# A decoder trunk on one core: slot counting, the router by token halves, and half of the gather ahead

## The reference

```python
def hierarchical_moe(h, w_rg, w_re, w_gate, w_up, w_down):
    t = h.reshape(-1, D)
    g_logits = (t @ w_rg).astype(F32)
    g_sel = jnp.argmax(g_logits, axis=-1)
    ...
    top_v, top_i = lax.top_k(e_in, TOP_K_IN_GROUP)
    e_w = jax.nn.softmax(top_v, axis=-1) * g_w
    ids = g_sel[:, None] * EXPERTS_PER_GROUP + top_i
    gates = jnp.einsum('nk,nke->ne', e_w, jax.nn.one_hot(ids, N_EXPERTS, dtype=F32))
    hg = jnp.einsum('nd,edf->nef', t, w_gate)
    hu = jnp.einsum('nd,edf->nef', t, w_up)
    act = (jax.nn.silu(hg.astype(F32)) * hu.astype(F32) * gates[..., None]).astype(t.dtype)
    y = jnp.einsum('nef,efd->nd', act, w_down)
    return y.reshape(B, S, D).astype(h.dtype)
```

## Time and profile before

| what | value |
|---|---|
| median of 3 runs | 1021.76 us (1020.68 to 1021.91) |
| the profiled execution | 1021.73 us |
| its span in the trace | 1019.8 us |
| mean granted TensorE clock | 0.996 of full speed |
| TensorE busy | 999.2 us, 98% of the span |
| VectorE busy | 477.2 us, 47% |
| DMA, mean over the span | 288 GB/s |

### The profile page before, as it was taken

One profiled execution on the slowest core, in us unless ns is written; L12 is line 12 of the kernel. 1 busy time (PEld: TensorE's weight loads), 2 busy tenths in 40 slices (PEclk: granted clock), 3 DMA queues, 4 the chain that ended last, 5 costly groups with the idle time before them and its releaser, 6 DMA issues.

```text
span 1019.8 us, 11159 instructions
## 1 busy us (share of the span) xinstructions
PE 999.2 (98%) x4494; PEld 547.1 (54%) x4494; DVE 477.2 (47%) x814; ACT 136.4 (13%) x323; POOL 98.8 (10%) x123
## 2 busy tenths in 40 slices
PE   8999999999999999999999999999999999999996
PEld 7657555669575454333334855565975433333332
DVE  2533375766554224432444636566655544444424
ACT  2211000411010010101112000032120010111111
POOL 3051032000010000000000512210000100000000
PEclk9999999999999999999999999999999999999999
DMA  9973000963379999999999420067385799999995
GB/s 359 425 299 131 35 0 6 409 249 123 125 277 391 406 423 421 419 423 420 421 420 420 163 82 1 1 254 285 148 327 193 297 421 420 421 420 421 421 415 220
DMA packets 44826, 293.58 MB, mean 288 GB/s; under 512 B 5472, under 2 KB 5728, under 8 KB 13024
## 3 DMA queue, kind: packets, MB, share of 16 engines
q1 hardware_dynamic: 38000, 266.36, 64.3%
q10 hardware_dynamic: 5616, 22.24, 5.6%
q0 software_dynamic: 1152, 4.19, 1.1%
HBM read 283.33 MB, written 9.44 MB: 287 GB/s over the span
## 4 chain that ended last, share of the span: by engine, by line
PE 89%; SPq 5%; DMA 3%; DVE 2%; issue 1%; POOL 0%; ACT 0%; DVEq 0%; POOLq 0%
PE bank L1001 18%; PE bank L1075 10%; PE bank L590 8%; PE bank L620 6%; PE bank L789 5%; PE bank L622 5%; PE bank L600 5%; PE bank L843 5%; PE bank L907 5%; SPq L512 5%; PE bank L693 5%; PE bank L1036 5%; PE bank L715 3%; DMA ring<-in_w_experts 3%; PE bank L580 2%; PE bank L877 1%
## 5 line engine op out<-in xcount | busy, mean ns | idle before, releaser
L1001 PE MATMUL bank<-ring,hT 128*64 128x512 f32 x704 | 195.0, 593 | 0.0
L1001 PEld LDWEIGHTS bank<-ring,hT 128*64 128x64 f32 x704 | 62.5, 137 | 87.2 <-issue 86.9
L590 PE MATMUL bank<-ring,hT 128*128 128x512 f32 x192 | 84.4, 592 | 0.0
L1937 DVE TENSOR_TENSOR x<-bank,x 128x512 f32<-128x512 f32 x64 | 44.3, 692 | 54.5 <-PE bank L1036 54.5
L1955 DVE TENSOR_SCALAR xs<-xs 128x512 f32<-128x512 f32 x8 | 3.4, 426 | 124.0 <-ACT xs L1315 124.0
L1036 PE MATMUL bank<-PT 128*128 128x512 f32 x128 | 59.2, 605 | 0.0
L1075 PE MATMUL bank<-ring,Vx 128*64 128x512 f32 x160 | 57.1, 596 | 1.4 <-DMA ring<-in_w_experts 1.3
L590 PEld LDWEIGHTS bank<-ring,hT 128*128 128x128 f32 x192 | 35.6, 190 | 40.2 <-issue 40.2
L1075 PE MATMUL bank<-ring,xs 128*64 128x512 f32 x224 | 56.7, 595 | 0.0
L600 PE MATMUL bank<-hT,ring 128*128 128x256 f32 x256 | 55.7, 379 | 0.8 <-DVE hT L1586 0.8
L789 PE MATMUL bank<-ring,hT 128*128 128x512 f32 x128 | 56.3, 595 | 0.1
(11 more groups left out here) (296 smaller groups left out, 1559.2 us busy)
## 6 DMA issues: line engine op xcount, KB each, us to landing
ring<-in_w_experts SPq DMA_DIRECT2D x146, 1024.0 KB, 15.0
ring<-in_w_mix SPq DMA_DIRECT2D x60, 1024.0 KB, 14.5
work<-in_w_experts SPq DMA_DIRECT2D x20, 1024.0 KB, 12.7
late<-in_w_experts SPq DMA_DIRECT2D x10, 1024.0 KB, 18.1
late<-in_w_mix ACTq DMA_DIRECT2D x4, 2048.0 KB, 10.0
keys<-in_w_experts SPq DMA_DIRECT2D x8, 1024.0 KB, 21.9
rot<-by_slot ACTq DMA_DIRECT2D x14, 512.0 KB, 8.0
by_slot<-late ACTq DMA_DIRECT2D x1, 4096.0 KB, 38.3
```

Of the source, the lines that this page charges most:

```text
L590: last = nc.tensor.matmul(b[:, :], lhs[:, c, m * P:(m + 1) * P], w[:, c, :], start=(c == 0), stop=(c == C - 1))
L1001: last = nc.tensor.matmul(banks[2 + g][b2 * CAP:(b2 + 1) * CAP, :], rows_T_of(p)[:, c, b2 * CAP:(b2 + 1) * CAP], w, start=(c == 0), stop=( ...
```

## The change

It has four parts.

1. The places of the first half are found as soon as its choice is there: one small matmul in a bank of its own (`rank0`, a new job) stands before p_3's last chunk and waits for `chosen` of half 0. VectorE scales the first half of `xs` at once, adds the base, and makes `slotf` and `hot` of half 0 ahead of the second choice (`slots`, `first_hot`, semaphore `r_first`).
2. The second half counts its places from the top end of each expert's 64 downwards (`top16` minus the count), so it doesn't need the first half's count; three matmuls are left in `rank`.
3. The gather is split by halves: the matmuls of half 0 run before and behind the `rank` matmuls, those of half 1 stay where the gather was. `keep_busy` gives one matmul in two places instead of two matmuls.
4. ScalarE's `first_loads` goes. The wait for the scatters stands behind the count of the first half slots and of gate, before pair 0's exponential, and the row loads of pairs 1 and 2 behind that exponential.

```diff
@@ job_list @@
-    jobs += [..., ("p_2", "D"), ("rt0", "D"), ("p_3", "D"), ("t5_10", "D"), ("t5_11", "D"), ("rt1", "D")]
+    jobs += [..., ("p_2", "D"), ("rt0", "D"), ("rank0", "D"), ("p_3", "D"), ("t5_10", "D"), ("t5_11", "D"), ("rt1", "D")]
@@ tensor @@
                 logits(0)
-                p_seventh("p_3")
+                NE = N_EXPERTS
+                p_seventh("p_3", range(3))
+                pe.wait_ge(chosen_done, 2 * L + 1)
+                b = open_bank(L, "rank0")
+                close(nc.tensor.matmul(b[:, 0:NE], before[:, :], chosen[:, 0, :], start=True, stop=True))
+                p_seventh("p_3", range(3, 4))
+
+                def gather(m, c2):
+
+                    b = banks[FIRST_ROWS[c2]]
+                    for k in range(4):
+                        last = nc.tensor.matmul(b[:, k * P:(k + 1) * P], xs[:, m, (4 * c2 + k) * P:(4 * c2 + k + 1) * P], hot[:, m, :],
+                                                start=(m == 0 and k == 0), stop=(m == 1 and k == 3), skip_group_check=True)
+                    return last
...
-                if L + 1 == DEPTH:
-                    wait_emptied(pe, L, BANK_BEFORE["router_kv0"])
-                keep_busy(2)
                 router_kv(0, range(2, 6))
+                pe.wait_ge(normed, 6 * L + 5)
+                pe.wait_ge(r_first[L], 1)
+                gather(0, 0)
+                keep_busy()
                 pe.wait_ge(chosen_done, 2 * L + 2)
                 b = open_bank(L, "rank")
-                NE = N_EXPERTS
-                nc.tensor.matmul(b[:, 0:NE], before[:, :], chosen[:, 0, :], start=True, stop=True)
-                nc.tensor.matmul(b[:, NE:2 * NE], before[:, :], chosen[:, 1, :], start=True, stop=False)
-                nc.tensor.matmul(b[:, NE:2 * NE], ones[:, :], chosen[:, 0, :], start=False, stop=True)
-                nc.tensor.matmul(b[:, 2 * NE:3 * NE], ones[:, :], chosen[:, 0, :], start=True, stop=False)
-                close(nc.tensor.matmul(b[:, 2 * NE:3 * NE], ones[:, :], chosen[:, 1, :], start=False, stop=True))
-
+                nc.tensor.matmul(b[:, 0:NE], before[:, :], chosen[:, 1, :], start=True, stop=True)
+                nc.tensor.matmul(b[:, NE:2 * NE], ones[:, :], chosen[:, 0, :], start=True, stop=False)
+                close(nc.tensor.matmul(b[:, NE:2 * NE], ones[:, :], chosen[:, 1, :], start=False, stop=True))
+
+                gather(0, 1)
+                keep_busy()
                 router_kv(0, range(6, C))
                 router_kv(1)
-                keep_busy(2)
...
                 for c2 in range(2):
-                    for k in range(4):
-                        for m in range(M):
-                            cols = xs[:, m, (4 * c2 + k) * P:(4 * c2 + k + 1) * P]
-                            last = nc.tensor.matmul(banks[FIRST_ROWS[c2]][:, k * P:(k + 1) * P], cols, hot[:, m, :], start=(m == 0), stop=(m == M - 1))
-                    routed_job(last)
+                    routed_job(gather(1, c2))
@@ scalar @@
-                def first_loads():
-                    act.wait_ge(r_sent[L], 16 * 2 * M)
-                    for p in (1, 2):
-                        load_rows(p)
-
...
                     units_read(p, "gate")
+                    if p == 0:
+                        act.wait_ge(r_sent[L], 16 * 2 * M)
                     nc.scalar.activation(rexp_of[L], banks[2][:, :], ACT.Exp, scale=-1.0).then_inc(r_gexp[L], 1)
+                    if p == 0:
+                        for q in (1, 2):
+                            load_rows(q)
                     units_read(p, "up")
...
-                either_way(act, L, routed, dense, first_loads, None, None, dense_last)
+                either_way(act, L, routed, dense, None, None, None, dense_last)
@@ vector @@
                 choose(0)
+                scale_tile(L, 2, 0)
+                wait_job(dve, L, "rank0")
+                emptied(V.tensor_tensor(rank[:, 0, :], base16, bank("rank0")[:, 0:N_EXPERTS], ALU.add))
                 p_sum("p_3", (1, 1))
...
+                wait_emptied(dve, L, "rank0")
+                slots(0)
                 wait_emptied(dve, L, "p_3")
                 rows_T("t5", 1, 24)
-                for m in range(M):
-                    scale_tile(L, 2, m)
+                scale_tile(L, 2, 1)
+                first_hot(0, r_first[L])
                 choose(1)
...
-                emptied(V.tensor_tensor(rank[:, :, :], bk[:, 0:2 * N_EXPERTS].rearrange("p (m n) -> p m n", m=M),
-                                        base16.unsqueeze(1).to_broadcast([P, M, N_EXPERTS]), ALU.add))
+                emptied(V.tensor_tensor(rank[:, 1, :], top16, bk[:, 0:N_EXPERTS], ALU.subtract))
                 wait_emptied(dve, L, "rank")
                 V.tensor_copy(most, mostf)
...
+                slots(1)
                 dve.sem_inc(flag_done, 1)
...
+                first_hot(1, r_hot[L])
```

More of the change, by code:

```diff
@@ L75, in job_list @@
     jobs += [(f"p_{i}", "D") for i in (7, 6, 5, 4)]
-    jobs += [("t5_00", "D"), ("t5_01", "D"), ("p_2", "D"), ("rt0", "D"), ("p_3", "D"), ("t5_10", "D"), ("t5_11", "D"), ("rt1", "D")]
+    jobs += [("t5_00", "D"), ("t5_01", "D"), ("p_2", "D"), ("rt0", "D"), ("rank0", "D"), ("p_3", "D"), ("t5_10", "D"), ("t5_11", "D"), ("rt1", "D")]
     return jobs + [("rank", "D")]
@@ L250, in trunk @@
         sm = sb("sm", [P, 112])
-        wsm = sb("wsm", [P, 242])
+        wsm = sb("wsm", [P, 258])
         early = PT[:, 2, 6:8, :].rearrange("p a t -> p (a t)")
@@ L346, in trunk @@
         r_hot = per_layer("r_hot")
+        r_first = per_layer("r_first")
         r_rowsT = per_layer("r_rowsT")
@@ L459, in trunk @@
         most = wsm[:, 241:242].bitcast(I32)
+        top16 = wsm[:, 242:258]
         one2 = PT[:, 1, 0, 0:64].rearrange("p (m k n) -> p m k n", m=M, k=2)
@@ L1883, in _, with slots, first_hot @@
                 choose(0)
+                scale_tile(L, 2, 0)
+                wait_job(dve, L, "rank0")
+                emptied(V.tensor_tensor(rank[:, 0, :], base16, bank("rank0")[:, 0:N_EXPERTS], ALU.add))
                 p_sum("p_3", (1, 1))
+                def slots(m):
+                    link(V.tensor_tensor(pick[:, m, :, :], one2[:, m, :, :], rank[:, m, :].unsqueeze(1).to_broadcast([P, 2, N_EXPERTS]), ALU.mult))
+                    link(V.tensor_reduce(slotf[:, m, :], pick[:, m, :, :], AX, ALU.add))
+                def first_hot(m, done):
+                    link(V.tensor_scalar(hot1[:, m, :], columns[:, :], slotf[:, m, 0:1], None, ALU.is_equal))
+                    V.scalar_tensor_tensor(hot[:, m, :], columns[:, :], slotf[:, m, 1:2], hot1[:, m, :], ALU.is_equal, ALU.add).then_inc(done, 1)
+                wait_emptied(dve, L, "rank0")
+                slots(0)
                 wait_emptied(dve, L, "p_3")
                 rows_T("t5", 1, 24)
-                for m in range(M):
-                    scale_tile(L, 2, m)
+                scale_tile(L, 2, 1)
+                first_hot(0, r_first[L])
                 choose(1)
@@ L1895, in _ @@
                 bk = bank("rank")
-                V.tensor_reduce(mostf, bk[:, 2 * N_EXPERTS:3 * N_EXPERTS], AX, ALU.max)
-                emptied(V.tensor_tensor(rank[:, :, :], bk[:, 0:2 * N_EXPERTS].rearrange("p (m n) -> p m n", m=M),
-                                        base16.unsqueeze(1).to_broadcast([P, M, N_EXPERTS]), ALU.add))
+                V.tensor_reduce(mostf, bk[:, N_EXPERTS:2 * N_EXPERTS], AX, ALU.max)
+                emptied(V.tensor_tensor(rank[:, 1, :], top16, bk[:, 0:N_EXPERTS], ALU.subtract))
                 wait_emptied(dve, L, "rank")
                 V.tensor_copy(most, mostf)
-                link(V.tensor_tensor(pick[:, :, :, :], one2[:, :, :, :], rank[:, :, :].unsqueeze(2).to_broadcast([P, M, 2, N_EXPERTS]), ALU.mult))
-                link(V.tensor_reduce(slotf[:, :, :], pick[:, :, :, :], AX, ALU.add))
+                slots(1)
                 dve.sem_inc(flag_done, 1)
                 V.tensor_copy(sloti, slotf[:, :, :].rearrange("p m k -> p (m k)")).then_inc(r_slots[L], 1)
-                inner = Chain(dve, r_chain[L])
-                for m in range(M):
-                    last = V.tensor_scalar(hot1[:, m, :], columns[:, :], slotf[:, m, 0:1], None, ALU.is_equal)
-                inner.link(last)
-                for m in range(M):
-                    last = V.scalar_tensor_tensor(hot[:, m, :], columns[:, :], slotf[:, m, 1:2], hot1[:, m, :], ALU.is_equal, ALU.add)
-                last.then_inc(r_hot[L], 1)
+                first_hot(1, r_hot[L])
                 dve.wait_ge(lexp_done, 2 * L + 2)
```

9 lines of the change are left out of this document (5 added, 4 removed).

## The result

The changed kernel took **1026.27 us** (median of five, 1025.4 to 1028.3) against 1021.91 for the kernel before it on the same chip: a ratio of 1.0042, 95% interval 1.0031 to 1.0054. That is 4.4 us slower, outside the predicted range. The profiled execution took 1027.07 us for a span of 1025.2.

A forecast was written before the change was run, and what follows sets the result against it. TensorE was taken to bound all before layer 1's end, the weight stream that end. 0.4 + 0.1 + 1.4 - 2.4 + 0.8 = +0.3 on 1021.73 gave 1022.0 us, range 1019.6 to 1024.3.

The forecast's parts named there:

- step 3: Layer 0: row loads issued behind the exponential land late, so TensorE waits 1.4 us for pair 1's rows (0.9 to 2.7).
- Step 1: p_3, both layers: TensorE waits for the first half's choice, 0.4 us paid in full (0.15 to 0.8).
- step 2: Layer 0's gather, split by halves: nearly a tie between VectorE and TensorE, 0.1 us lost (0 to 0.3).
- Step 4: Layer 1: weights follow the scatter without a stop, gate and up start 1.4 earlier; gain 2.4 us (1.6 to 3.0).
- Step 5: Layer 1: rank matmul and scatter come 0.8 us later (0 to 1.3), with the granted clock at half.
- Step 6: Layer 1: late rows and exponential may cost TensorE 2 us, hidden; from a loss of 2.5 it would decide.
- C: Rival: row loads queue behind weights in both layers, 2.7 us in layer 0, 4.0 in layer 1; 1024.8 us, chance 0.15.
- A: Rival: layer 0's row loads land in time, so no wait for them; 1020.6 us, chance 0.12.
- B: Rival: rows in time or at low bound, clock stays up in layer 1's router; 1019.8 or 1019.2 us, chance 0.13.
- D: Rival: layer 1's end is not the DMA's, only TensorE's part counts; +0.5 us, chance 0.05.

The follow-up runs named there:

- a1: The changed kernel with layer 0's row loads of pairs 1 and 2 back ahead of the first half count, layer 1 as changed: 1021.68 us.
- d1: The changed kernel with layer 0's half and gate counts of the first pair both behind the row loads, issued at the same moment: 1021.02 us.
- b1: The changed kernel with twelve filler matmuls ahead of TensorE's wait for pair 1's rows in layer 0: 1032.01 us.
- b3: a1 with layer 1's exponential ahead of the wait for the scatter and the row loads behind it: 1022.11 us.
- b4: b3 with both first slots of layer 1 counted free only behind the exponential: 1021.80 us.
- c1: The changed kernel with four filler matmuls ahead of TensorE's wait for pair 1's rows in layer 0: 1025.80 us.
- c2: The changed kernel with layer 0's gate count behind the row loads, which are issued at the same moment: 1024.68 us.
- c3: The changed kernel with only pair 1's row load behind layer 0's exponential, and pair 2's behind the count for up: 1025.11 us.
- b5: b3 with pair 1's row transposes behind pair 0's down projection in layer 1: 1021.79 us.
- e2: The changed kernel with d1's layer 0 and b5's layer 1: 1021.98 us.
- a2: The changed kernel with ScalarE's order as before the change in both layers, so the router and gather part alone: 1021.81 us.
- e1: The changed kernel with d1's layer 0 and b4's layer 1: 1022.15 us.
- a3: The kernel before the change with the ScalarE part of the change alone: 1025.66 us.
- a4: The changed kernel with the scatter wait and row loads between the half's count and gate's count, in both layers: 1022.30 us.

## Why the prediction was wrong

In the medians the forecast was off by 4.1: +4.4 came instead of +0.3. a1 divides it. The late row loads cost 4.6 (1026.27 less 1021.68) where step 3 gave 1.4, and all the rest was worth 0.0 where the other steps gave -1.1.

**Step 1** (p_3 waits 0.4) and **step 2** (gather, +0.1) were right within their bounds: 0.3 together in layer 0, 0.2 of it in p_3.

**Step 3** (layer 0's row loads) failed, in size. The mechanism, the place and the waiting instruction were as forecast, but 1.4 us were 3.5, and 1.6 more of clock behind it, for which the step had no term: 5.1 against 1.4 in the profiled execution, and that is the greater part of the miss. The landing was priced at 8.0 with 9.3 as the upper bound, and it took 10.2; in the other kernels with the loads at this place and all counts ahead it took 8.9 to 10.6, the waits that no filler covered being 2.4 to 3.9. The 8.0 came from the pair at 310.46, which the step counted among loads issued while weights stream. No expert weights were out then, the first went out at 315.45; what these two had ahead was one load of 2 MB of mixing weights on ScalarE's own queue, issued at 308.25. Only the 9.3 came from beside the stream. d1 shows the lateness to be the work of the counts ahead; why it is 10.2 and not 8 or 9.3 stays open. The Trainium skill's formula in "DMA: Bandwidth & Descriptors", section "Anatomy of one DMA — SWDGE (gpsimd) path", gives an estimate of 3.2 for such a load. The page states it for DMAs issued from GpSimd, and these go out on ScalarE's queue. d1's 4.2 with nothing ahead comes within 1 us of it; the 10.2 of the changed kernel disagrees.

**Step 4** (the hole closed, -2.4) failed too, in its worth. The hole did close: no slice between scatter and stream is as empty as those of the earlier trace rows. But gate and up began only 0.5 earlier instead of 1.4 (803.99 against 799.66, less 4.8). One slice at a share of 1.14 moved only 250 GB/s, so full engines were not full rate; that this is the scatter's doing isn't shown, for the kernel before has 250 GB/s at a share of 0.96 from 806 to 807, where its weights begin and no scatter is left. With 50 MB to come the gain was 0.8, where steps 4 and 5 together gave 1.6. And "it arrives whole at the last chunk" was wrong: the last load landed 5.4 later than before, not 4.0, behind the two microseconds of a single engine. The early start also cost TensorE VectorE's stop. The end of layer 1 has two chains close together: in ten of the kernels, the one before and the changed one among them, the end lies 12.8 behind the last weight load's landing, and in the other seven (a1, b1, b3, b4, c1, c2, c3) 12.9 to 14.4, with TensorE's chain last. So moving one of them alone shows little, and a1, b3, b5 and e2 all come out level with the kernel before.

**Step 5** (the scatter +0.8, the clock at half around the first gather) was right, at the edge of its bounds: the rank matmul stands at 799.33, 6.06 later than before, less 4.8 is 1.3, of 0 to 1.3, and the clock stands at 0.50:

```profile
794.00:796.00 2.00, 2.00 (x12) 2.00 (x13) 1.11 (x4) 0.00 (x0) 0.00 (x0) 0.57 0.96 397
796.00:798.00 2.00, 2.00 (x9) 1.97 (x10) 1.72 (x12) 0.00 (x0) 0.00 (x0) 0.50 0.99 418
798.00:800.00 2.00, 2.00 (x7) 0.77 (x6) 1.07 (x9) 1.13 (x6) 0.00 (x0) 0.50 0.42 176
```

**Step 6** (a loss of up to 2 us in layer 1, hidden) erred twice and came out near: the loss on TensorE was 2.9, over the 2.5 from which it said it would decide, and it came through VectorE, which no step named (2.1 of wait and 1.3 of half clock behind it, less the 0.5 by which gate and up began earlier). The waits for weights at the end shrank from 2.7 to 1.3, as it should if TensorE's chain had caught up.

**The rivals.** C came nearest: row loads delayed by the weights beyond the forecast; it gave 1024.8 and 0.15. Its price of 2.7 for layer 0 was still below 3.5, it had no clock, and in layer 1 the rows were not what TensorE waited for first. It held itself less likely on the ground of the pair at 310.46, which had no expert weights beside it when it was issued. A, B and D are out: rows late, and in a2 a gain of 2.1 on TensorE hidden by the weights.

## What to carry to other kernels

A small load that something waits for belongs ahead of the count that lets a big stream go, not behind it: the same two loads, issued at the same moment, landed in 4.2 and 5.0 us with the counts behind them, and in 10.2 and 13.6 with the counts ahead. When a landing time is read from a trace for another place, read with it what else was in the engines at that issue, and of which queue. A gain in a stream's middle is not yet one at its end: look at when its last load lands. And where two chains end together, first show by one experiment each that mending one alone moves the end, before anything is built on it.

## What the runs showed of the hardware

- A 512 KB load issued with no weight load out landed in 4.1 to 4.9 us (d1, e1, e2); with 3 to 12 loads of 1 MB out, in 7.7 to 10.2 (the changed kernel, the first of each pair), and 12 made it no later than 3. Beside the stream its queue moved nothing for some 4 us and then had a third of the engines' time.
- VectorE stood still for 3.6 to 6.2 us at its branch in every kernel. In five kernels, all with the weights out before its block in layer 1, it stood still a second time there, for 3.5 to 4.8 us; in a3, with the weights out before as well, it didn't. In a1, a4, b1, c1, c2 and c3 its exponential came too late to tell.
- The granted clock fell to 0.50 for some 3 us behind waits of 3.54, 3.89, 2.53 and (layer 1) 2.07 us, not behind waits of 2.36 and 2.99, and not where fillers ran in the wait.
- A 128x512 float32 product took 0.86 us in the fillers, in two records of 0.43: a record is not an instruction.
- A share near 1 is not full rate: 250 GB/s at 1.14 (scatter ending, weights beginning) and at 0.96 (weights beginning, no scatter), where weights alone move 421.
- The last 2 us of the changed kernel's stream ran at a share of 0.06 and 25 GB/s, one engine of sixteen; the kernel before had 33 GB/s in its last microsecond and 209 in the one before it.
